# Second attention's rotary partners by DMA, first attention's reciprocals, slab quarters and parts in other places

## The chip, the cores and the metric

The kernel runs on one core of a Trainium2 chip, in one launch. The metric is the time on the device in microseconds (us): the median of three runs was 1079.1 us (1078.55 to 1080.32).

## The reference

Two blocks are computed on 256 tokens of width 1024, in float32. The first has a token mixer (sparse attention with a key selector, 8 heads, beside a short gated convolution), layer norms and a SwiGLU; its shifts, scales and gates come from `c_act @ w_ada`, a vector times a 1024x6144 matrix. The second has two layers: a gated linear attention, then a differential attention, each followed by a SwiGLU and a gated projection. The two places that the change touches:

```python
# first block, attention of the token mixer (8 heads, keys and values shared)
logits = jnp.where(valid, einsum('bqhd,bqkd->bhqk', q_b, kg) * attn_scale, NEG_INF)
p = softmax(logits); out = einsum('bhqk,bqkd->bqhd', p, vg)

# second block, layer 1: differential attention, 8 heads of 2 x 64
q = rms_norm(q.reshape(b, s, nh, 2, dh), g_q)          # k alike
q = rope(q), k = rope(k)                               # x1*cos - x2*sin, x2*cos + x1*sin
s = einsum('bhtqd,bhtkd->bhtqk', q_blk, kt) * dh ** -0.5
pr = softmax(s); a = pr[:, :, 0] - lam * pr[:, :, 1]
o = einsum('bhqk,bhkd->bhqd', a, vt)
```

## The kernel before

Activations lie transposed in SBUF: 128 features on the partitions, 256 tokens along the row, so 1024 features are eight tiles of 128x256. A weight matrix comes in *slabs* of 128x4096 words (2 MB), over two raw buffers. Most projections are made in three products: `split` on ScalarE (line 890) copies a quarter of a slab into the rounded type (`whi`), `low` on VectorE (line 1458) subtracts that from the raw slab (`wlo`), and `three` on TensorE (line 2217) multiplies high by high, high by low and low by high. A slab of four tiles is 96 matmuls.

Each engine has one program, written out by hand in order, and the engines meet at semaphores alone. `me.next(sem)` waits for one more count of a semaphore, `wait_ge` for a count, `banks.claim(bank, sem)` on TensorE waits until the last reader of a PSUM bank is done. There is no planner: what stands behind a waiting instruction on its engine waits too. SyncE's queue loads weights in the order of the phases, with the loads of `behind` (line 672) between them, in order.

**First attention (the head loop at lines 1717 to 1739 on VectorE, 1103 to 1117 on ScalarE, 2517 to 2532 on TensorE).** For head i TensorE makes the scores of head i+1, then one tile of another projection (`in_hc` in heads 0 to 3, `in_gb` in heads 4 to 7), transposes the probabilities of head i (`turned`), multiplies them with the values of head i-1, and sometimes sums columns for the modulation. VectorE does `masked_maxima` (mask, row maxima), ScalarE the exponentials with their sums, VectorE the reciprocals (`invert_sums`), ScalarE the scaling. Between these VectorE has filling work: the convolution of a tile, `low` quarters of the slabs of `out0`, and `modulate_part(n)`, which multiplies a 128x1024 part of `w_ada` (512 KB) into an accumulator. The parts' buffers are reused: in SyncE's order the load of part 20 waits until part 18 is used up (line 638, `part_used` at 19), and behind part 20 stand `load_out(1)`, the second slab of `out0`, and parts 21 to 23. The first quarter of that slab is split by ScalarE in head 5, ahead of its copy of the transposed probabilities.

**Second attention.** `diff_q` and `diff_k` are two slabs each; a slab gives two *pairs* r of tiles (r = 0 to 7; 0 to 3 are q). VectorE takes each tile out of PSUM (line 1997), ScalarE squares a pair (line 1371), TensorE sums the squares over each half of 64 partitions (`block_sums`, line 2767, a 128x512 float32 matmul), ScalarE makes the root (`roots`), VectorE normalizes (line 2122). The rotary partner of a row is 32 partitions away: `partners` (line 2773) multiplies the pair with a signed permutation `rot_d` into PSUM. GpSimd multiplies the pair with the cosines (line 859), and VectorE in `turn(r)` multiplies the partners with the sines and adds (lines 2128, 2132). `partners(r-2)`, `partners(r-1)` and their turns stand one slab later, behind tiles 1 and 3; the last two stand in the middle of the first value tile.

Then a loop over eight heads runs beside the value projection (`value_steps`, three matmuls each, line 2812 to 2862): scores of head i+1, attend(i-2), six value steps, transposes(i-1). VectorE makes maxima, probabilities and `low` quarters, ScalarE exponentials, copies and `split` quarters (`ahead`, line 1429); `ahead(*OUT2, 0)` waits until the second value tile is done.

Of the kernel before, what the change touches and what calls it, by code (L numbers as in the profile page):

```python
# [24 lines left out]
ALU = mybir.AluOpType  # L25
# [39 lines left out]
def column_of(rows):  # L65
    at, n = {}, 0
    for name, k in rows:
# [9 lines left out]
CONSTS = [("ident", P), ("rot_q", P), ("rot_i", P), ("cos_q", T), ("sin_q", T), ("cos_i", T), ("sin_i", T),  # L77
          ("causal", 3 * P), ("blk", P), ("rot_d", P), ("cos_d", T), ("sin_d", T), ("gla_mask", 2 * P)]
COL_C, NC = column_of(CONSTS)
# [3 lines left out]
def shape_constants():  # L83

    out = np.zeros((P, NC), np.float32)

    def put(name, a):
        out[:, COL_C[name]:COL_C[name] + a.shape[1]] = a

    p = np.arange(P)  # L90
    put("ident", np.eye(P))
    put("blk", (p[:, None] // HD == p[None, :] // HD) * 1.0)
    pos = np.arange(T, dtype=np.float32)
    for tag, width, half, theta in (("q", HD, 8, 500000.0), ("i", ID, 8, 500000.0), ("d", HD, 32, 10000.0)):
# [9 lines left out]
        put("rot_" + tag, rot)  # L104
# [168 lines left out]
def build(nc, a, out):  # L273

    ctx = ExitStack()
    with ctx:
# [110 lines left out]
        d_sq, d_rs = sb("d_sq", 1024, at=U + 8192), sb("d_rs", 1024, at=U + 9216)  # L387
        d_t1, d_t2 = sb("d_t1", 512, at=U + 10240), sb("d_t2", 512, at=U + 10752)
        d_nsq = sb("d_nsq", 2048, at=U)
# [6 lines left out]
        def sem(name):  # L396
# [56 lines left out]

        qk_src, qk_sq, qk_stat, qk_sd, qk_normed, qk_cos, qk_rot, qk_rot_read, qk_ready = (
            sem("qk_src"), sem("qk_sq"), sem("qk_stat"), sem("qk_sd"), sem("qk_normed"), sem("qk_cos"),
            sem("qk_rot"), sem("qk_rot_read"), sem("qk_ready"))
        out_done, out_read, last_read, stored = sem("out_done"), sem("out_read"), sem("last_read"), sem("stored")
# [411 lines left out]
        def _(act):  # L869
# [491 lines left out]
            root(X[0], T + 2, 1.0 / D, 1, rstd[:, :])  # L1361
            take_projection(3)
            for base, name in ((0, "diff_q"), (4, "diff_k")):
                def after(at, t, base=base):
                    buf = d_q if base == 0 else d_k
                    if t % 2 == 1:
                        r = base + 2 * at.i + t // 2
# [21 lines left out]
            for q in range(4):  # L1389
                ahead(*VALUES, q)  # L1390
            take_values(0)

# [8 lines left out]
            for i in range(NH + 1):  # L1401
# [24 lines left out]
                if i in (2, 5, 7):  # L1426
                    take_values({2: 1, 5: 2, 7: 3}[i])
                if 1 <= i <= 4:
                    ahead(*OUT2, i - 1)
            wait(act, tile_done, PH["diff_v"].tile0 + 4)  # L1430
# [24 lines left out]
        def _(dve):  # L1455
# [259 lines left out]

            PARTS_OF_HEAD = ((11, 12), (13, 14), (15, 16), (17, 18), (19, 20), (21,), (22,), (23,))
            me.again()
            masked_maxima(0)
            for q in range(2):
                low(PH["out0"], At(0), q)  # L1720
            modulate_part(10)
            for i in range(NH):
                invert_sums(i)
                if i + 1 < NH:
# [3 lines left out]
                if i == 7:  # L1728
                    mix_low(0, 1)
                if i in (1, 2):  # L1730
                    low(PH["out0"], At(0), i + 1)
                if i < 4:
                    short_conv(i)
                else:
                    gated_conv(i - 4)
                    if i in (5, 6):
                        low(PH["out0"], At(1), i - 5)
                for n in PARTS_OF_HEAD[i]:
# [386 lines left out]
            def turn(r):  # L2125
                me.next(qk_rot)
                me.again(qk_ready)
                me.did(dve.tensor_tensor(v3(d_t2[:, :], 2), v3(X[2 + r % 2][:, :], 2), bc(C("sin_d", T), 2), ALU.mult),
                       qk_rot_read)
                me.next(qk_cos)  # L2130
                me.again(qk_rot_read)
                me.did(dve.tensor_tensor(pair(r), d_t1[:, :], d_t2[:, :], ALU.add), qk_ready)

# [12 lines left out]
            low(*VALUES, 0)  # L2146
            low(*VALUES, 1)
            turn(6)
            turn(7)
            make_tile = group_make(d_o, d_nsq, lambda t: lam[:, 5:6])  # L2150
# [10 lines left out]
            for i in range(NH + 3):  # L2161
                if i < NH:
                    me.next(score_done)
                    s = 4 * (i % 2)
                    for c in range(2):
                        me.did(dve.tensor_reduce(neg_max[:, s + 2 * c:s + 2 * c + 2],
                                                 v3(G[2 * (i % 2) + c][:, :], 2), AX, ALU.max, negate=True))
                    me.again()
                    me.did(dve.tensor_scalar(neg_max[:, s:s + 4], neg_max[:, s:s + 4], HD ** -0.5, None, ALU.mult),
                           max_ready)  # L2170
                if i >= 3:
# [22 lines left out]
                if i in (0, 1):  # L2194
                    low(*VALUES, 2 + i)
                if 2 <= i <= 5:
                    low(*OUT2, i - 2)
            for g in range(1, 4):
# [14 lines left out]
        def _(pe):  # L2213
# [554 lines left out]

            def partners(r):
                banks.claim(X[2 + r % 2], qk_rot_read)  # L2770
                pe.wait_ge(qk_normed, r + 1)
                src = tl(d_q, 2 * r, 2) if r < 4 else tl(d_k, 2 * r - 8, 2)
                pe.matmul(X[2 + r % 2][:, :], C("rot_d"), src, start=True, stop=True).then_inc(qk_rot, 1)  # L2773

            start = next_operand()
            for base, name in ((0, "diff_q"), (4, "diff_k")):
                def after(at, t, base=base):
                    r = base + 2 * at.i
                    if r == 0 and t == 1:
                        stats(tok=True)  # L2780
                    if t == 1 and r:
                        partners(r - 2)
                    if t == 3:
                        if r:
                            partners(r - 1)
                        block_sums(r)
# [19 lines left out]

            value_steps(0, 8)
            partners(6)
            partners(7)
            value_steps(8, 16)  # L2810

# [88 lines left out]
```

## Time and profile before

| | |
|---|---|
| median of 3 runs | 1079.1 us (1078.55 to 1080.32) |
| profiled execution, its own time | 1077.96 us |
| its span | 1076.2 us |
| TensorE (PE) busy | 1042.4 us, 97% |
| VectorE (DVE) busy | 731.7 us, 68% |
| ScalarE (ACT) busy | 552.9 us, 51% |
| GpSimd (POOL) busy | 202.2 us, 19% |
| mean granted TensorE clock | 0.995 |

The span is the time from the first to the last instruction of that execution. Rows of a timeline give an instruction's start and its length in us, its engine, line and operands, how many like it are merged, and in brackets how long the engine sat idle before and what ended that. PEld is the weight load of TensorE; SPq and ACTq are DMAs issued by SyncE and ScalarE. Each float32 matmul stands as two records.

### The profile page before, as it was taken

How to read it: one execution, taken by the hardware profiler on the slowest of the kernel's cores; microseconds unless marked ns; L12 is line 12 of the kernel's file. 1: busy time of each engine (PE TensorE's matmuls, PEld its weight loads, DVE VectorE, ACT ScalarE, POOL GpSimd, SP SyncE). 2: the span in 40 equal slices, each digit the busy share in tenths (PEclk: the TensorE clock that was granted, in tenths of full speed). 3: DMA queues.
4: the chain of work that ended last, by engine and by line, in shares of the span. 5: the costliest groups of instructions: out<-in, count | busy, mean ns of one | idle time of the engine just before them, and what ended most of it. 6: DMA issues, size and time to landing. Idle time of an engine off the chain costs nothing.

```text
span 1076.2 us, 20430 instructions
## 1 busy us (share of the span) xinstructions
PE 1042.4 (97%) x7993; PEld 981.9 (91%) x7993; DVE 731.7 (68%) x1155; ACT 552.9 (51%) x946; POOL 202.2 (19%) x223
## 2 busy tenths in 40 slices
PE   5999999999999999999999999999989999999998
PEld 5577788999999998989999999998877999999998
DVE  5798777767654788868556555686787765564565
ACT  2223457545363585527454444566467764544453
POOL 0000012233311001022333321021210223322010
PEclk9999999999999999999999999999999999999999
DMA  9993453577556454504564546654322265644661
GB/s 350 399 389 121 169 184 98 195 254 262 174 168 190 137 192 173 183 2 153 186 209 156 174 131 203 247 185 157 131 105 79 93 222 178 212 132 140 185 208 40
DMA packets 183587, 192.78 MB, mean 179 GB/s; under 512 B 5913, under 2 KB 143426, under 8 KB 183522
## 3 DMA queue, kind: packets, MB, share of 16 engines
q1 hardware_dynamic: 182512, 191.15, 52.5%
q8 instruction: 43, 0.70, 0.3%
q0 software_dynamic: 144, 0.52, 0.2%
q10 hardware_dynamic: 866, 0.21, 0.1%
q14 instruction: 22, 0.18, 0.0%
HBM read 190.83 MB, written 1.05 MB: 178 GB/s over the span
## 4 chain that ended last, share of the span: by engine, by line
PE 56%; DVE 5%; ACT 3%; issue 1%; POOL 0%; DVEq 0%; POOLq 0%; ACTq 0%
PE gemm L2219 17%; PE gemm L2221 17%; PE gemm L2220 16%; DVE wlo L1464 1%; PE aux L2717 1%; PE aux L2835 1%; PE aux L2767 1%; ACT whi L899 1%; DVE prod L1943 1%; PE gemm L2820 1%; PE aux L2773 0%; PE aux L2219 0%; DVE state L2075 0%; PE aux L2221 0%; PE aux L2220 0%
## 5 line engine op out<-in xcount | busy, mean ns | idle before, releaser
L2219 PE MATMUL gemm<-ohi,whi 128*128 128x256 f32 x1376 | 389.5, 283 | 3.8 <-issue 1.1
L1464 DVE TENSOR_TENSOR wlo<-raw,whi 128x1024 fp32r<-128x1024 f32 (+1 forms) x308 | 352.2, 1187 | 58.8 <-ACT whi L899 58.1
L2220 PE MATMUL gemm<-olo,whi 128*128 128x256 f32 x1376 | 385.8, 280 | 0.0
L2221 PE MATMUL gemm<-ohi,wlo 128*128 128x256 f32 x1376 | 383.6, 279 | 0.0
L899 ACT ACTIVATE whi<-raw 128x1024 fp32r<-128x1024 f32 (+1 forms) x308 | 276.4, 963 | 60.4 <-PE gemm L2221 44.2
L2219 PEld LDWEIGHTS gemm<-ohi,whi 128*128 128x128 f32 x1376 | 259.1, 188 | 6.7 <-DVE wlo L1464 2.8
L2220 PEld LDWEIGHTS gemm<-olo,whi 128*128 128x128 f32 x1376 | 259.5, 189 | 0.6 <-issue 0.5
L2221 PEld LDWEIGHTS gemm<-ohi,wlo 128*128 128x128 f32 x1376 | 259.4, 189 | 0.0
L2221 PE MATMUL gemm<-acthi,wlo 128*128 128x256 f32 x528 | 147.8, 280 | 0.0
L2219 PE MATMUL gemm<-acthi,whi 128*128 128x256 f32 x528 | 147.5, 279 | 0.0
L2220 PE MATMUL gemm<-actlo,whi 128*128 128x256 f32 x528 | 147.3, 279 | 0.0
L755 POOL TENSOR_TENSOR prod<-sg,ut 128x256 f32<-128x256 f32 x66 | 51.2, 777 | 265.1 <-DVE ut L1888 161.0
L2220 PEld LDWEIGHTS gemm<-actlo,whi 128*128 128x128 f32 x528 | 99.3, 188 | 0.0
L2221 PEld LDWEIGHTS gemm<-acthi,wlo 128*128 128x128 f32 x528 | 99.1, 188 | 0.0
L2219 PEld LDWEIGHTS gemm<-acthi,whi 128*128 128x128 f32 x528 | 98.8, 187 | 0.0
L1194 ACT ACTIVATE sg<-gt 128x256 f32<-128x256 f32 x66 | 27.6, 419 | 132.9 <-DVE gt L1888 91.4
L759 POOL TENSOR_TENSOR actlo<-prod,acthi 128x256 f32 (+1 forms) x63 | 70.3, 1116 | 0.0
L2220 PE MATMUL gemm<-xlo,whi 128*128 128x256 f32 x224 | 62.6, 279 | 0.0
L1888 DVE TENSOR_TENSOR ut<-gemm,rstd 128x256 f32<-128x256 f32 x44 | 18.4, 418 | 52.1 <-PE gemm L2221 52.1
L782 POOL TENSOR_TENSOR sq_sum<-sq_sum,dsq 128x256 f32<-128x256 f32 x28 | 24.0, 856 | 111.3 <-ACT dsq L924 99.2
L2220 PEld LDWEIGHTS gemm<-xlo,whi 128*128 128x128 f32 x224 | 42.2, 188 | 1.9 <-issue 1.9
L2448 PE MATMUL gemm<-om,raw 128*128 128x256 f32 x192 | 43.6, 383 | 0.0
(383 smaller groups left out, 1549.0 us busy)
## 6 DMA issues: line engine op xcount, KB each, us to landing
raw<-in_ffn_w_in SPq DMA_DIRECT2D x44, 1024.0 KB, 6.2
raw<-in_ffn_w_out SPq DMA_DIRECT2D x32, 704.0 KB, 5.2
part<-in_w_ada SPq DMA_DIRECT2D x32, 512.0 KB, 10.7
raw<-in_gla_w_in SPq DMA_DIRECT2D x6, 2048.0 KB, 7.8
raw<-in_diff_w_in SPq DMA_DIRECT2D x6, 2048.0 KB, 7.9
raw<-in_w_gate SPq DMA_DIRECT2D x11, 1024.0 KB, 6.3
raw<-in_w_up SPq DMA_DIRECT2D x11, 1024.0 KB, 8.5
raw<-in_w_down SPq DMA_DIRECT2D x16, 704.0 KB, 5.2
```

The costliest lines, as they stand in the source:

```text
L755: pool.tensor_tensor(tl(prod, j), tl(sg, j), tl(ut, j), ALU.mult).then_inc(prod_done, 1)
L759: pool.tensor_tensor(tl(actlo, t - 1), tl(prod, 1 - j), tl(acthi, t - 1).bitcast(F32), ALU.subtract).then_inc(actlo_ready, 1)
L782: pool.tensor_tensor(sq_sum[:, :], sq_sum[:, :], src, ALU.add).then_inc(squares_summed if last else sq_added, 1)
L899: act.activation(whi[hslot][:, q * w:(q + 1) * w], src[:, q * w:(q + 1) * w], ACT.Copy).then_inc(hi_ready, 1)
L1194: act.activation(tl(sg, j), tl(gt, j), ACT.Silu).then_inc(silu_done, 1)
L1464: dve.tensor_tensor(wlo[hslot][:, q * w:(q + 1) * w], src[:, q * w:(q + 1) * w], whi[hslot][:, q * w:(q + 1) * w].bitcast(F32), ALU.subtra ...
L1888: ins = dve.tensor_tensor(dst, bank[:, 0:T], rstd[:, 0:T], ALU.mult)
L1943: me.link(dve.tensor_tensor(tl(prod, t % 2), tl(sg, t % 2), pp(k, t), ALU.mult))
L2219: pe.matmul(dst, st_hi, mv_hi, start=start, stop=False)
L2220: pe.matmul(dst, st_hi, mv_lo, start=False, stop=False)
L2221: return pe.matmul(dst, st_lo, mv_hi, start=False, stop=stop_)
L2448: ins = pe.matmul(G[t][:, 0:T], w[:, k, t * P:(t + 1) * P], tl(om, k), start=k == 0, stop=k == KT - 1)
```

## The change

1. `partners` and the matrix `rot_d` go. For each pair r ScalarE issues four DMAs of 32 partitions x 512 words (64 KB each) that copy the pair from SBUF to SBUF with neighbouring groups of 32 partitions exchanged; the sign moves into the table of sines. Pairs r-2 and r-1 are moved behind the first tile of the next slab, pairs 6 and 7 behind the second quarter of the last value slab's `ahead`. VectorE's `turn` waits for the DMA and multiplies in SBUF.
2. In the second attention the maxima of head 0 stand between `turn(6)` and `turn(7)`; the quarters of the first slab of `out2` are split in heads 2 to 5 (before 1 to 4) and their low parts made in heads 3 to 6 (before 2 to 5).
3. In the first attention `invert_sums(i+1)` stands behind head i's convolution or gate, where `invert_sums(i)` stood at the start of head i; that of head 0 stands between the two quarters before the loop. The third quarter stays out of head 1 and goes to head 2, the fourth from head 2 to head 4. From part 12 on, each part up to 20 is made one place later: heads 0 to 7 make (11), (12, 13), (14, 15), (16, 17), (18, 19), (20, 21), (22), (23), where they made (11, 12), (13, 14), (15, 16), (17, 18), (19, 20), (21), (22), (23).

```diff
+            def move_partners(r):
+                src = tl(d_q, 2 * r, 2) if r < 4 else tl(d_k, 2 * r - 8, 2)
+                act.wait_ge(qk_normed, r + 1)
+                if r >= 2:
+                    act.wait_ge(qk_ready, r - 1)
+                for b in range(4):
+                    act.dma_start(d_rot[r % 2][32 * b:32 * b + 32, :], src[32 * (b ^ 1):32 * (b ^ 1) + 32, :]).then_inc(
+                        qk_moved[r % 2], 16)
...
+                    if t == 0 and base + at.i:
+                        for r in (base + 2 * at.i - 2, base + 2 * at.i - 1):
+                            move_partners(r)
...
             for q in range(4):
                 ahead(*VALUES, q)
+                if q == 1:
+                    move_partners(6)
+                    move_partners(7)
...
-                if 1 <= i <= 4:
-                    ahead(*OUT2, i - 1)
+                if 2 <= i <= 5:
+                    ahead(*OUT2, i - 2)
...
-            PARTS_OF_HEAD = ((11, 12), (13, 14), (15, 16), (17, 18), (19, 20), (21,), (22,), (23,))
+            PARTS_OF_HEAD = ((11,), (12, 13), (14, 15), (16, 17), (18, 19), (20, 21), (22,), (23,))
             me.again()
             masked_maxima(0)
-            for q in range(2):
-                low(PH["out0"], At(0), q)
+            low(PH["out0"], At(0), 0)
+            invert_sums(0)
+            low(PH["out0"], At(0), 1)
             modulate_part(10)
             for i in range(NH):
-                invert_sums(i)
                 if i + 1 < NH:
                     masked_maxima(i + 1)
...
-                if i in (1, 2):
-                    low(PH["out0"], At(0), i + 1)
                 if i < 4:
                     short_conv(i)
                 else:
                     gated_conv(i - 4)
-                    if i in (5, 6):
-                        low(PH["out0"], At(1), i - 5)
+                if i + 1 < NH:
+                    invert_sums(i + 1)
+                if i in (2, 4):
+                    low(PH["out0"], At(0), 1 + i // 2)
+                if i in (5, 6):
+                    low(PH["out0"], At(1), i - 5)
                 for n in PARTS_OF_HEAD[i]:
                     modulate_part(n)
...
             def turn(r):
-                me.next(qk_rot)
-                me.again(qk_ready)
-                me.did(dve.tensor_tensor(v3(d_t2[:, :], 2), v3(X[2 + r % 2][:, :], 2), bc(C("sin_d", T), 2), ALU.mult),
-                       qk_rot_read)
+                rot = d_rot[r % 2]
+                dve.wait_ge(qk_moved[r % 2], 64 * (r // 2 + 1))
+                me.did(dve.tensor_tensor(v3(rot[:, :], 2), v3(rot[:, :], 2), bc(C("sin_d", T), 2), ALU.mult), qk_turned)
...
             turn(6)
+            maxima(0)
             turn(7)
...
-                if 2 <= i <= 5:
-                    low(*OUT2, i - 2)
+                if 3 <= i <= 6:
+                    low(*OUT2, i - 3)
...
-                    if t == 1 and r:
-                        partners(r - 2)
                     if t == 3:
-                        if r:
-                            partners(r - 1)
                         block_sums(r)
                         block_sums(r + 1)
...
-            value_steps(0, 8)
-            partners(6)
-            partners(7)
-            value_steps(8, 16)
+            value_steps(0, 16)
```

## Rows read from the trace of the kernel before

**Rows 1.** The page, busy time of TensorE

```profile
PE 1042.4 (97%) x7993; PEld 981.9 (91%) x7993; DVE 731.7 (68%) x1155; ACT 552.9 (51%) x946; POOL 202.2 (19%) x223
```

**Rows 2.** Windows: us, busy by engine (PE, PEld, DVE, ACT, POOL), clock, DMA share, GB/s

```profile
806.00:808.00 2.00, 2.00 (x7) 1.46 (x5) 1.96 (x5) 2.00 (x8) 0.00 (x0) 0.50 0.03 8
```

**Rows 3.** Timeline of TensorE, one partner matmul in diff_q

```profile
742.11 1.02 PE L2773 MATMUL aux<-d_q,const 128*128 128x512 f32 x2
742.56 0.68 PE L2219 MATMUL gemm<-dhi,whi 128*128 128x256 f32 x1
743.08 0.28 PE L2220 MATMUL gemm<-xlo,whi 128*128 128x256 f32 x1
743.20 0.28 PE L2221 MATMUL gemm<-dhi,wlo 128*128 128x256 f32 x1
```

**Rows 4.** Timeline of all engines, from the first slab's end to the second's

```profile
734.74 0.63 ACT L1371 ACTIVATE d_sq<-d_q 128x512 f32<-128x512 f32 x1 [0.27 <-DVE d_q L1997]
735.48 0.30 PEld L2767 LDWEIGHTS aux<-d_sq,const 128*128 128x128 f32 x2 [0.60 <-issue]
...
738.03 1.42 DVE L2122 SCALAR_TENSOR_TENSOR d_q<-d_q,cols_b,d_rs 128x512 f32<-128x512 f32 x2 [3.33 <-ACT d_rs L963]
...
743.07 2.34 DVE L1464 TENSOR_TENSOR wlo<-raw,whi 128x1024 fp32r<-128x1024 f32 x2
...
748.61 1.02 PE L2773 MATMUL aux<-d_q,const 128*128 128x512 f32 x2
...
749.27 0.63 ACT L1371 ACTIVATE d_sq<-d_q 128x512 f32<-128x512 f32 x1 [2.85 <-DVE d_q L1997]
749.47 1.88 PE L2767 MATMUL aux<-d_sq,const 128*128 128x512 f32 x4
```

**Rows 5.** ScalarE's DMA issues in its timeline, and KB and us to landing of two transfers

```profile
23.62 0.36 ACTq L987 DMA_DIRECT2D lam_in<-in_diff_lam_q  x1
...
25.01 0.58 ACT L983 ACTIVATE om<-res,mod 128x256 f32<-128x256 f32 x1
...
lam_in<-in_diff_lam_k ACTq DMA_DIRECT2D x2, 32.0 KB, 6.6
...
out<-o_tok SPq DMA_DIRECT2D x4, 256.0 KB, 2.6
```

**Rows 6.** Timeline of all engines, first heads of the second attention

```profile
788.28 0.84 ACT L1385 ACTIVATE d_v<-gemm,rstd 128x256 f32<-128x256 f32 x2 [1.75 <-PE gemm L2221]
...
792.00 0.47 ACT L1409 ACTIVATE d_p<-gemm,neg_max 128x256 f32<-128x256 f32 x1 [2.87 <-DVE neg_max L2169]
...
794.07 1.13 PE L2820 MATMUL gemm<-d_k,d_q 64*128 64x256 f32 x8 [1.32 <-ACT d_p L1409]
...
801.54 1.06 ACT L899 ACTIVATE whi<-raw 128x1024 fp32r<-128x1024 f32 x1 [2.95 <-PE aux L2221]
...
804.57 1.78 PE L2820 MATMUL gemm<-d_k,d_q 64*128 64x256 f32 x8 [1.91 <-ACT d_p L1409]
...
806.27 2.07 PE L2835 MATMUL aux<-d_pt,d_v 128*128 128x256 f32 x4
```

**Rows 7.** TensorE's waits in the whole span: us in total, times, longest

```profile
PE aux L2501 <- ACT logit L1075: 2.8, 3, 1.3
```

**Rows 8.** Timeline of the first attention, heads 3 to 6, and out_w's landing

```profile
117.23 0.17 DVE L1714 RECIPROCAL rsum<-sums 128x2 f32<-128x2 f32 x1
...
117.63 0.47 SPq L657 DMA_DIRECT2D out_w<-in_w_out  x1
...
126.70 1.04 ACT L899 ACTIVATE whi<-out_w 128x1024 fp32r<-128x1024 f32 x1
...
130.57 0.56 DVE L1704 SCALAR_TENSOR_TENSOR logit<-aux,allow 128x384 f32<-128x384 f32 x1
...
133.46 1.10 PE L2333 MATMUL gemm<-mix_sq,const 128*128 128x512 f32 x2 [0.32 <-ACT mix_sq L1069]
...
DMA to landing us min/median/max: 8.7/8.8/9.0
```

More of the change, by code:

```diff
@@ L77 @@
 CONSTS = [("ident", P), ("rot_q", P), ("rot_i", P), ("cos_q", T), ("sin_q", T), ("cos_i", T), ("sin_i", T),
-          ("causal", 3 * P), ("blk", P), ("rot_d", P), ("cos_d", T), ("sin_d", T), ("gla_mask", 2 * P)]
+          ("causal", 3 * P), ("blk", P), ("cos_d", T), ("sin_d", T), ("gla_mask", 2 * P)]
 COL_C, NC = column_of(CONSTS)
@@ L103, in shape_constants @@
                 cos[m], sin[m] = np.cos(ang[d % half]), np.sin(ang[d % half])
-        put("rot_" + tag, rot)
+        if tag == "d":
+            sin *= rot.sum(0)[:, None]
+        else:
+            put("rot_" + tag, rot)
         put("cos_" + tag, cos)
@@ L387, in build @@
         d_sq, d_rs = sb("d_sq", 1024, at=U + 8192), sb("d_rs", 1024, at=U + 9216)
-        d_t1, d_t2 = sb("d_t1", 512, at=U + 10240), sb("d_t2", 512, at=U + 10752)
+        d_t1 = sb("d_t1", 512, at=U + 10240)
+        d_rot = [sb(f"d_rot{i}", 512, at=place["ohi"] + 512 * i) for i in range(2)]
         d_nsq = sb("d_nsq", 2048, at=U)
@@ L452, in build @@
             sem("u_read"), sem("go_done"), sem("go_read"), sem("gated"))
-        qk_src, qk_sq, qk_stat, qk_sd, qk_normed, qk_cos, qk_rot, qk_rot_read, qk_ready = (
+        qk_src, qk_sq, qk_stat, qk_sd, qk_normed, qk_cos, qk_turned, qk_ready = (
             sem("qk_src"), sem("qk_sq"), sem("qk_stat"), sem("qk_sd"), sem("qk_normed"), sem("qk_cos"),
-            sem("qk_rot"), sem("qk_rot_read"), sem("qk_ready"))
+            sem("qk_turned"), sem("qk_ready"))
+        qk_moved = [sem("qk_moved0"), sem("qk_moved1")]
         out_done, out_read, last_read, stored = sem("out_done"), sem("out_read"), sem("last_read"), sem("stored")
@@ L2125, in turn @@
             def turn(r):
-                me.next(qk_rot)
-                me.again(qk_ready)
-                me.did(dve.tensor_tensor(v3(d_t2[:, :], 2), v3(X[2 + r % 2][:, :], 2), bc(C("sin_d", T), 2), ALU.mult),
-                       qk_rot_read)
+                rot = d_rot[r % 2]
+                dve.wait_ge(qk_moved[r % 2], 64 * (r // 2 + 1))
+                me.did(dve.tensor_tensor(v3(rot[:, :], 2), v3(rot[:, :], 2), bc(C("sin_d", T), 2), ALU.mult), qk_turned)
                 me.next(qk_cos)
-                me.again(qk_rot_read)
-                me.did(dve.tensor_tensor(pair(r), d_t1[:, :], d_t2[:, :], ALU.add), qk_ready)
+                me.again(qk_turned)
+                me.did(dve.tensor_tensor(pair(r), d_t1[:, :], rot[:, :], ALU.add), qk_ready)
             for base, name in ((0, "diff_q"), (4, "diff_k")):
@@ L2147, in _, with maxima @@
             low(*VALUES, 1)
+            def maxima(i):
+                me.next(score_done)
+                s = 4 * (i % 2)
+                for c in range(2):
+                    me.did(dve.tensor_reduce(neg_max[:, s + 2 * c:s + 2 * c + 2],
+                                             v3(G[2 * (i % 2) + c][:, :], 2), AX, ALU.max, negate=True))
+                me.again()
+                me.did(dve.tensor_scalar(neg_max[:, s:s + 4], neg_max[:, s:s + 4], HD ** -0.5, None, ALU.mult),
+                       max_ready)
             turn(6)
+            maxima(0)
             turn(7)
@@ L2161, in _ @@
             for i in range(NH + 3):
[L2162 to L2170, printed above, removed]
+                if 1 <= i < NH:
+                    maxima(i)
                 if i >= 3:
@@ L2767, in block_sums @@
                 pe.matmul(X[r % 2][:, :], C("blk"), tl(d_sq, r % 2, w=512), start=True, stop=True).then_inc(qk_stat, 1)
[L2769 to L2773, printed above, removed]
             start = next_operand()
```

## Prediction, made before the change was run

> **What bounds the kernel now.** I read the page first, for the share of each engine: TensorE is busy for 97% of the span [rows 1], so work taken off TensorE counts in full unless something else becomes late, and anything put between its instructions costs in full. Second, TensorE's waits: where it stands still, there is something to win or to lose. Third, the timelines of the three stretches that the change touches: the first attention (85 to 140 us), the projections of q and k (734 to 780 us) and the heads of the second attention (788 to 834 us). Last the windows, for the granted clock. The reader is to see four things.
>
> A partner product costs TensorE 0.86 us. It starts at 742.11 and the second product behind it at 743.08 [rows 3]. Products follow each other at 0.12 us (743.08 to 743.20), so without it the second would start at 742.23: a difference of 0.85.
>
> The second attention has two stalls on TensorE, 1.32 and 1.91 us, both for ScalarE's exponentials [rows 6]. Behind the longer one the clock is at 0.50, 1.2 instead of 2.4 GHz [rows 2], and the scores take 1.78 us where they took 1.13, the product with the values 2.07 us [rows 6].
>
> The first attention has three stalls, 2.8 us together, in which TensorE waits for scaled probabilities [rows 7].
>
> And in the first attention there is a chain that costs nothing today only because it just arrives: part 18 is used up at 117.23, the second slab of `out0` is issued behind part 20's load at 117.63, lands 8.7 to 9.0 us later, at 126.3 to 126.6, and ScalarE splits it at 126.70 [rows 8].
>
> **Partners by DMA.** Eight products go: 8 x 0.855 = 6.8 us. Not all of it is kept. At the end of a slab the second `block_sums` needs the squares of the pair that ended last. In the first slab it starts 0.11 us behind the end of the squares (734.74 + 0.63 = 735.37, then 735.48) [rows 4]. In later slabs the partner product covers this: tile 3 ends at 748.61, the squares at 749.27 + 0.63 = 749.90, and the sums run from 749.47 on without a wait [rows 4]. Without the cover the first sum takes 748.61 to 749.47 and the second waits until 750.01, 0.54 us. That happens in three slabs, 1.6 us. Left: 6.8 - 1.6 = 5.2 us.
>
> What the DMAs add. ScalarE issues 32 of them at about 0.36 us each [rows 5]; eight in a slab are 2.9 us. The instruction before an issue may still be running: a DMA that stands behind four activations is issued at 23.62, while the last of them runs at 25.01 [rows 5]. So the issues begin when VectorE has normalized the first of the two pairs (738.03 + 0.71, 4.6 us after the slab's end at 734.1 [rows 4]), beside the first two split quarters of 1.0 us each, and end at about 7.6 us; there the third quarter starts. VectorE takes that quarter at 743.07 [rows 4], 9.0 us after the slab's end, so nothing is late. This cover is 0.4 us; if the issues take longer or begin only when the quarters are done, the third starts at 9.2 us, VectorE is up to 1.2 us late, and in three slabs 3.6 us are lost. VectorE turns a pair behind the fourth quarter, at 743.07 + 2.34 [rows 4], 11.3 us after the slab's end. No copy from SBUF to SBUF is in the trace. Nearest from below is the store of 256 KB with 2.6 us, from above the 32 KB with 6.6 us in the saturated start [rows 5]. I take 2.6 us, from the row with idle engines; in the slabs 11.3 us are enough for 6.0 + 2.6 as they are, and for the first pair nearly with 6.6 too. Behind the last slab it matters: pair 6 is issued 4.6 to 6 us after the slab's end and its turn can come at 8.7, behind two quarters; with 2.6 us it lands in time, with 6.6 us everything up to the first exponentials is about 4 us later, and some 2 to 4 of these reach TensorE.
>
> The Trainium skill, "DMA: Bandwidth & Descriptors", section "Issuing engines are not separate DMA queues", says that DMAs issued by ScalarE and SyncE run on the same 16 engines and interleave. By that rule the last two moves share with the 2 MB that SyncE issues about 5 us earlier; its effect lies inside the bounds above.
>
> **Quarters and maxima of the second attention.** `ahead(*OUT2, 0)` waits for the second value tile, until 801.54, and holds back the exponentials of head 2, for which TensorE stands 1.91 us [rows 6]. Moved behind these, it holds back nothing: the exponentials of head 2 can run when their maxima are there. The stall goes, and with it the slow clock: 1.78 - 1.13 and 2.07 - 1.13, 1.6 us; I take 1.5. What is late next: with the partner products gone TensorE reaches the scores at 782.8 (5.35 us earlier), the scores of head 1 need the bank of the first value tile, and ScalarE's copy of it (788.28 [rows 6]) now stands behind eight issues and two splits and ends at 785.4. TensorE waits some 1.6 us there, in place of the 1.32 us at 794.07. The exponentials of head 0 start at about 786.4 instead of 792.00, since the maxima no longer wait for `turn(7)`. From head 3 on TensorE is 8.0 to 8.4 us earlier than before; VectorE, with 4.9 us per head against TensorE's 4.7, keeps up, since it has lost its wait for the split. The low quarters one head later delay the second slab of `out2` by nothing (that load waits for the value slab) and the next feed-forward load not beyond its old time. Sum of the second attention: 5.2 + 1.9 + 1.5, less 0.3 for the changed first stall and 0.3 for waits of ScalarE and VectorE = **-8.0 us**. From below -9.5 (no new stalls), from above -4 (slow copies or 2.9 us of issues uncovered).
>
> **Reciprocals, quarters and parts of the first attention.** TensorE no longer waits in heads 0 to 3: the reciprocal stands a whole head ahead. By head 5 that brings it 3.5 us forward (2.8 us of waits and about 0.2 us around each). But part 18, on which the second slab of `out0` depends, moves from the second place of head 3 to the first of head 4. Ahead of it stand now, besides what stood there, the maxima of head 5 (1.1 us), the gate (0.35), the wait for the exponentials of head 5, since the reciprocal follows a short gate (0.7), two more reciprocals (0.2) and 0.7 us of VectorE's waits for a TensorE that is no longer late: 117.2 + 3.1 = 120.3. The slab's load is issued at 120.7 and lands at 129.5 with the 8.8 us of [rows 8]. ScalarE comes to the split at 125.4 and stands for 4 us; behind it stand its copy of head 5's probabilities and the scaling of head 6. VectorE stands at the low quarter of the same slab and has behind it two parts instead of one. Split until 130.6 (1.04 us [rows 8]), low until 131.9 (1.17 us [rows 4]), parts 20 and 21 until 134.8, then the maxima of head 7, which began at 130.57 [rows 8]. Exponentials, squares of the gated tiles, sums: 137.6 instead of 133.46 [rows 8]. So the first attention ends 4.0 us later, with the 3.5 us gained in it already spent. TensorE stands from 128.3 to 132.0 and from 133.3 to 137.6; a wait of 1.9 us was enough for the slow clock, and there it lasted over 3 us, from the scores at 804.57 to 808 [rows 2, 6], which is half as much in lost work: I take 1.7 us more. Nothing later in the kernel gives this back: TensorE is busy without a break from there to the layer norm. Sum: **+5.7 us**; from below -3.5 (the load arrives in time), from above +8.
>
> The smaller table of constants (64 KB less) and VectorE's product, which reads SBUF in place of PSUM, I put at nothing; both are under 0.2 us.
>
> **Sum.** 1077.96 - 8.0 + 5.7 = 1075.7 us for the profiled execution. The median of the runs is 1.1 us above that execution, so 1076.8 us for the median. A measurement of this kernel can tell about 0.2%, 2.2 us, from no change; the forecast is 2.3 us faster and lies at that bound.
>
> **The rivals.**
>
> *The late slab does not hold anything up (1068 us).* Then the first attention gives its 3.5 us: -8.0 - 3.5 = -11.5, so 1067.6. For it: the three waits [rows 7] really go. Against it: the load is bound to part 18 by SyncE's order, and today it has under half a microsecond to spare [rows 8].
>
> *The moves are late or the issues hold ScalarE up (1080.8 us).* From the point at which a copy takes over 4 us, pair 6 is late for `turn(6)`, all maxima and exponentials of the heads shift, and where the issues lie in front of the third quarter uncovered, 3.6 us go in the slabs. Either takes 4 of the 8 us, and with +5.7 the kernel is slower: 1079.1 - 4 + 5.7 = 1080.8. For it: 6.6 us for 32 KB [rows 5]. Against it: that row is from a time with saturated DMA engines.
>
> *The clock falls again, in the second attention or for longer in the first (1079 us).* TensorE stands 1.6 us behind the first scores, between 1.32 us that cost no clock and 1.91 us that did [rows 6]; price 1.5 us, and a longer slow stretch in the first attention another 1 us: 1076.8 + 2.5 = 1079.3.
>
> *The change does not do what it says*, in that the moved partners or the wait at head 2 stay on the path: the trace would show products of line 2773 or the 1.91 us wait; the code leaves no room for either.
>
> **How the numbers follow.** The forecast has 0.45; with its own range of 1074 to 1079 it is faster by over 0.2% in 0.25, the same in 0.17, slower in 0.03. The first rival has 0.22, faster. The late moves have 0.17: slower in 0.13, same in 0.04. The clock has 0.16: same in 0.07, slower in 0.09. Faster 0.47, same 0.28, slower 0.25. The range from 1067.5 to 1082 holds all cases but the ends of the first and third.
>
> **What would show it.** Right: no products of the rotation; `block_sums` with a wait of about 0.5 us for the squares in three slabs; the 1.91 us wait and the clock of 0.50 at 806 us gone; a wait of ScalarE for `out_w` of about 4 us in head 5, a wait of TensorE for it behind, and a clock of 0.50 around 138 us. Wrong: `out_w` issued at about 117 us or landing before ScalarE comes to it; a `turn` that waits for its DMA; the first attention ending earlier than before.

## The result and the profile after

The changed kernel takes 1086.4 us (median of 4 runs, 1085.35 to 1087.87), the kernel before 1078.8 us beside it. The ratio is 1.0071, 95% interval 1.0058 to 1.0084: 0.7% slower. The forecast was 1076.8 with a range up to 1082, so both the sign and the range were wrong. One run of a later kernel (e10 below) took 5175.8 us; it is left out of that kernel's ratio.

The page of the changed kernel, its busy times and the chain that ended last:

```profile
PE 1039.1 (96%) x7977; PEld 980.2 (90%) x7977; DVE 733.8 (68%) x1155; ACT 552.5 (51%) x946; POOL 202.1 (19%) x223
...
PE 53%; DVE 6%; ACT 4%; ACTq 2%; issue 1%; DVEq 0%
```

The waits of TensorE in the two edited stretches (us in total, times, longest; the first two rows from the heads of the first attention, the others from the second attention):

```profile
PE gemm L2362 <- ACT mix_sq L1074: 4.4, 1, 4.4
PE aux L2530 <- ACT logit L1080: 3.4, 1, 3.4
...
PE aux L2796 <- ACT d_sq L1390: 5.0, 6, 1.2
PE gemm L2836 <- ACT d_v L1404: 4.3, 1, 4.3
```

TensorE has less work than before [rows 1] (7977 records against 7993: the eight partner products, of two records each, are gone) and the kernel is longer: new waits have replaced it. The three waits of [rows 7] are gone, and so is the 1.91 us of [rows 6]. What is new on the chain is ACTq, ScalarE's own issues of DMAs, with 2% of the span, some 20 us of chain (0% on the page of the kernel before).

To see where the 7.4 us of span (1076.2 to 1083.6) arise I followed the lag at fixed places of the program. The weight load that SyncE issues at 83.89 us before goes out at 85.51 after: 1.6 us, ahead of any edited instruction. The last transposes of the first attention lag 6.8 us; the first tile of `diff_q` 5.6 (1.2 us were given back on the way, in small steps between 185 and 300 us, in code that the change does not touch; the trace of e3 below, whose first attention is the same, gives nothing back there); the last product with the values 7.6, the end 7.4. So: 1.6 early, 5.2 in the first attention, 1.2 back, and 2.0 in the second attention, which was to give 8.0.

The timeline of the changed kernel in the first attention (start, length, engine, line, operands, count, idle time before and its cause):

```profile
122.30 0.47 SPq L662 DMA_DIRECT2D out_w<-in_w_out  x1
131.03 1.06 ACT L904 ACTIVATE whi<-out_w 128x1024 fp32r<-128x1024 f32 x1 [4.11 <-DMA out_w<-in_w_out]
132.12 1.22 DVE L1486 TENSOR_TENSOR wlo<-out_w,whi 128x1024 fp32r<-128x1024 f32 x1 [6.23 <-ACT whi L904]
133.30 0.52 PE L2530 MATMUL aux<-const,logit 128*128 128x128 f32 x3 [3.36 <-ACT logit L1080]
136.14 0.56 DVE L1726 SCALAR_TENSOR_TENSOR logit<-aux,allow 128x384 f32<-128x384 f32 x1
139.03 2.05 PE L2362 MATMUL gemm<-mix_sq,const 128*128 128x512 f32 x2 [4.42 <-ACT mix_sq L1074]
```

Against [rows 8] the slab of `out0` is issued 4.7 us later (1.6 of them were there at 85 us already); ScalarE stands 4.1 us for it, VectorE behind it, and TensorE twice. The sums took 1.10 us and take 2.05: the slow clock.

The same view for one slab of the second attention, from the first slab's sums to the second's:

```profile
740.22 1.99 PE L2796 MATMUL aux<-d_sq,const 128*128 128x512 f32 x4 [0.38 <-ACT d_sq L1390]
744.42 0.61 ACTq L1376 DMA_DIRECT2D d_rot<-d_q  x1
744.98 1.04 ACT L904 ACTIVATE whi<-raw 128x1024 fp32r<-128x1024 f32 x1
748.26 1.76 ACTq L1376 DMA_DIRECT2D d_rot<-d_q  x2
750.07 2.01 ACT L904 ACTIVATE whi<-raw 128x1024 fp32r<-128x1024 f32 x2 [4.05 <-issue]
751.16 2.36 DVE L1486 TENSOR_TENSOR wlo<-raw,whi 128x1024 fp32r<-128x1024 f32 x2 [2.41 <-ACT whi L904]
754.66 1.10 PE L2796 MATMUL aux<-d_sq,const 128*128 128x512 f32 x2 [1.16 <-ACT d_sq L1390]
756.72 2.05 PE L2796 MATMUL aux<-d_sq,const 128*128 128x512 f32 x2 [0.96 <-ACT d_sq L1390]
```

The eight issues run from 744.42 to 750.02, 5.6 us, partly beside the first two splits, and the third quarter waits 4.05 us for them ("issue": it waited for no other engine). VectorE then has both last quarters, the third tile and the turn in one heap, the squares are late and TensorE waits twice. The sums start 14.4, 16.0 and 15.0 us apart in the three slabs; before it was 14.9, 14.7 and 14.7 with the partner products between them.

All issues of the moves, as a group (ns min/median/max), and their landing:

```profile
L1376 ACTq DMA_DIRECT2D d_rot<-d_q x16: 515/612/1117, 744.4 to 765.4; - x16
L1376 ACTq DMA_DIRECT2D d_rot<-d_k x16: 514/612/1520, 776.0 to 796.3; - x16
DMA to landing us min/median/max: 2.0/2.1/3.0
```

An issue takes 0.61 us in the median, not the 0.36 of [rows 5]; the copy is on time but for one turn, for which VectorE waits 0.8 us. At the end of the last slab the same happens ahead of the values (ScalarE, then TensorE):

```profile
796.96 2.00 ACT L904 ACTIVATE whi<-raw 128x1024 fp32r<-128x1024 f32 x2 [4.36 <-issue]
798.87 0.82 ACT L1404 ACTIVATE d_v<-gemm,rstd 128x256 f32<-128x256 f32 x2
799.84 2.08 PE L2836 MATMUL gemm<-d_k,d_q 64*128 64x256 f32 x8 [4.33 <-ACT d_v L1404]
```

The granted clock in windows of the changed kernel (columns as in [rows 2]) is 0.50 from 798 to 804 us, TensorE having stood still from 795.5:

```profile
798.00:800.00 2.00, 0.16 (x2) 0.20 (x3) 1.86 (x4) 2.00 (x6) 0.72 (x1) 0.50 0.00 0
802.00:804.00 2.00, 2.00 (x10) 2.00 (x11) 1.93 (x7) 0.52 (x3) 0.00 (x0) 0.50 0.00 0
```

### The profile page after: what moved, and what is told of

It reads as the page before. It is cut to its first block, busy times and chain, and to the rows that moved or that the text cites. A ratio compares the mean times of both kernels' runs of the same rounds, so it can differ in the third digit from the quotient of the medians.

```text
span 1083.6 us, 20418 instructions
## 1 busy us (share of the span) xinstructions
PE 1039.1 (96%) x7977; PEld 980.2 (90%) x7977; DVE 733.8 (68%) x1155; ACT 552.5 (51%) x946; POOL 202.1 (19%) x223
## 4 chain that ended last, share of the span: by engine, by line
PE 53%; DVE 6%; ACT 4%; ACTq 2%; issue 1%; DVEq 0%
PE gemm L2248 15%; PE gemm L2250 15%; PE gemm L2249 15%; DVE wlo L1486 2%; ACTq L1376 2%; ACT whi L904 1%; PE aux L2746 1%; PE aux L2851 1%; PE gemm L2836 1%; PE aux L2248 1%; PE aux L2796 1%; DVE prod L1967 1%; PE aux L2250 1%; PE aux L2249 1%; DVE state L2099 0%
## 5 line engine op out<-in xcount | busy, mean ns | idle before, releaser
L2477 PEld LDWEIGHTS gemm<-om,raw 128*128 128x128 f32 x192 | 36.5, 193 | 8.5 <-issue 3.8
## 6 DMA issues: line engine op xcount, KB each, us to landing
part<-in_w_ada SPq DMA_DIRECT2D x32, 512.0 KB, 10.4
```

The source lines that it names most:

```text
L2477: ins = pe.matmul(G[t][:, 0:T], w[:, k, t * P:(t + 1) * P], tl(om, k), start=k == 0, stop=k == KT - 1)
```

## Experiments

Every kernel was timed against the kernel before on the same chip; ratios are with their 95% intervals. "Second attention" is the time in its profile from the first tile of `diff_q` to the last product with the values; it repeats within 1.1 us where the code of that stretch is the same.

| kernel | us | ratio to before | second attention |
|---|---|---|---|
| before | 1078.8 | 1 | 103.5 |
| after | 1086.4 | 1.0071 | 105.5 |
| e1 second attention only | 1081.6 | 1.0015 | 105.9 |
| e2 first attention only | 1085.2 | 1.0064 | 103.5 |
| e3 half the issues | 1077.5 | 0.9992 | 96.1 |
| e4 moves by SyncE | 1075.7 | 0.9977 | 95.2 |
| e5 old parts | 1079.7 | 1.0006 | 105.5 |
| e6 late parts on before | 1083.5 | 1.0041 | 103.5 |
| e7 quarters, maxima on before | 1075.3 | 0.9964 | 99.7 |
| e8 e4 and e5 | 1069.2 | 0.9908 | 95.1 |
| e9 e8, norm behind gate | 1069.9 | 0.9917 | 95.1 |
| e10 slab before part 20 | 1083.1 | 1.0034 | 104.9 |
| e11 double issues | 1109.0 | 1.0277 | 128.8 |
| e12 e9, low quarters later | 1067.9 | 0.9896 | 95.1 |

**e1 and e2: the halves of the change.** e1 has the edits of the second attention alone, e2 those of the first.

> The second attention's edits alone (moves by DMA, maxima, quarters of out2); the first attention as in the kernel before. Theory A: the two stretches are independent, and the second attention is a small loss: from the first tile of diff_q to the last head the changed kernel lost 2.0 us more (5.6 us behind at diff_q's first tile, 7.6 behind at the last product with the values), so this kernel is 2 us slower than before, 1080.8 us. If the 1.6 us that the changed kernel was behind already at 85 us come from the smaller table of constants, they show here too: 1082.4. Rival B: the second attention gains its 8 us when it is alone, and the loss came from the two together: 1071.

> The first attention's edits alone (reciprocals, quarters, parts); partners on TensorE, maxima and out2's quarters as before. Theory A: 5.6 us slower at diff_q's first tile less the 1.6 us that were there at 85 us, ahead of any edited instruction: 4.0 us slower, 1082.8; if these 1.6 us come from this part of the change, 5.6 us slower, 1084.4. Rival: the delay is given back later in the kernel, 1079 to 1080.

e1: 1081.6 us, 1.0015 (1.0002 to 1.0027), second attention 105.9. e2: 1085.2, 1.0064 (1.0051 to 1.0078), second attention 103.5. The halves add up (0.15% + 0.64% against 0.71%), rival B falls, and the first attention's delay is still there at the end: e2's span is 5.9 us longer than that of before. The early 1.6 us belong to neither: e6, with the table of constants of before, has them (its load goes out at 85.25), and e3, with the smaller table, has not (83.80). In these kernels they go with the granted clock from 35 to 45 us. Four kernels in that window, in order before, after, e6, e3:

```profile
35.00:45.00 10.00, 8.81 (x30) 5.12 (x31) 6.58 (x13) 4.03 (x6) 0.00 (x0) 0.83 1.05 412
```
```profile
35.00:45.00 10.00, 8.81 (x27) 4.67 (x26) 6.58 (x13) 3.99 (x5) 0.00 (x0) 0.66 1.05 410
```
```profile
35.00:45.00 10.00, 8.81 (x25) 4.67 (x25) 6.67 (x13) 3.99 (x5) 0.00 (x0) 0.66 1.05 411
```
```profile
35.00:45.00 10.00, 8.81 (x30) 5.03 (x30) 6.67 (x13) 4.11 (x6) 0.00 (x0) 0.83 1.05 411
```

In e5, e8, e10 and e11 the load is late too (84.87 to 85.46) with 0.83 to 1.00 in that window. There a group of 32 products that starts at 24.2 to 24.4 us takes 10.1 to 11.4 us in place of 8.43, while the clock column shows 1.00; why, the traces do not show. So this time comes and goes in code that is the same, and it needs no edit. Whether the change makes it more frequent is open: one of the four profiled executions with the old table has it, and eight of the ten with the smaller one.

**e3: half the issues, the same bytes.**

```diff
-                src = tl(d_q, 2 * r, 2) if r < 4 else tl(d_k, 2 * r - 8, 2)
+                src = tl(d_q, 2 * r, 4) if r < 4 else tl(d_k, 2 * r - 8, 4)
...
-                    act.dma_start(d_rot[r % 2][32 * b:32 * b + 32, :], src[32 * (b ^ 1):32 * (b ^ 1) + 32, :]).then_inc(
-                        qk_moved[r % 2], 16)
+                    act.dma_start(d_rot_both[32 * b:32 * b + 32, :], src[32 * (b ^ 1):32 * (b ^ 1) + 32, :]).then_inc(
+                        qk_moved[0], 16)
...
-                        for r in (base + 2 * at.i - 2, base + 2 * at.i - 1):
-                            move_partners(r)
+                        move_partners(base + 2 * at.i - 2)
```

> The changed kernel with both pairs of a slab moved by the same four DMAs (32 partitions x 1024 words, 128 KB) in place of eight of 64 KB: half the issues, the same bytes. Theory A: what holds the third quarter of a slab back is ScalarE's time for issues, 0.61 us each and 4.9 us for eight; with four the third quarter starts 2.4 us earlier in each slab, the waits for squares fall from 5.0 us to about 1.6 and the wait of 4.3 us ahead of the scores of head 1 to about 2, with less slow clock: 6 to 8 us faster than the changed kernel, 1079 to 1080. Rival C: an issue takes twice as long for twice the bytes, or the waits come from the partner product's missing cover alone: within 1 us of the changed kernel, 1086.

1077.5 us, 0.9992 (0.9983 to 1.0001): 8.9 us faster than the changed kernel, a little more than expected. Second attention 96.1. An issue of twice the bytes costs the same, and the waits for squares are 1.6 us in four:

```profile
L1377 ACTq DMA_DIRECT2D d_rot<-d_q x8: 515/612/620, 745.6 to 761.2; - x8
```
```profile
PE aux L2795 <- ACT d_sq L1390: 1.6, 4, 0.4
PE gemm L2835 <- ACT d_v L1404: 1.5, 1, 1.5
```

**e11: twice the issues, the same bytes.**

```diff
-                for b in range(4):
-                    act.dma_start(d_rot[r % 2][32 * b:32 * b + 32, :], src[32 * (b ^ 1):32 * (b ^ 1) + 32, :]).then_inc(
+                for b in range(8):
+                    act.dma_start(d_rot[r % 2][16 * b:16 * b + 16, :], src[16 * (b ^ 2):16 * (b ^ 2) + 16, :]).then_inc(
```

> The changed kernel with each move cut into eight DMAs of 16 partitions (32 KB) in place of four of 64 KB: 64 issues, the same bytes. Theory A: ScalarE pays about 0.6 us for each issue, whatever its size (e3: 0.61 for 128 KB); 16 issues between the second and the third quarter are 9.8 us, the third quarter starts 4.9 us later in three slabs, and the scores of head 1 wait 4.9 us longer for ScalarE's copy: 20 us slower than the changed kernel, 1104 to 1110. Rival C: the time goes with the bytes: 1086 to 1088.

1109.0 us, 1.0277 (1.0263 to 1.0291), second attention 128.8: 22.6 us slower than the changed kernel, as expected. ScalarE's third quarter in the first slab:

```profile
758.01 2.00 ACT L904 ACTIVATE whi<-raw 128x1024 fp32r<-128x1024 f32 x2 [9.75 <-issue]
```

With 0, 16, 32 and 64 issues on ScalarE (e4, e3, after, e11) the second attention takes 95.2, 96.1, 105.5 and 128.8 us: the first 16 are nearly free, the next cost 0.6 us each and more, since the cover is used up. One detail was not as expected: the wait ahead of the scores (8.0 us) was for the turned pair, not for ScalarE's copy.

**e4: the same moves issued by SyncE.**

```diff
+                      ("diff_k", 0): moves(0, 1), ("diff_k", 1): moves(2, 3),
+                      ("diff_v", 0): moves(4, 5), ("diff_v", 1): moves(6, 7),
```

> The changed kernel with the same 32 DMAs issued by SyncE, each group of eight behind the weight load that is issued at the same slab's end. Theory A: ScalarE's queue is free again, so the third quarter starts as before; the second attention gives the forecast's 8 us in place of a loss of 2: 10 us faster than the changed kernel, 1076 to 1078. Rival C: the moves' landing or the missing cover is the cause, and it stays at 1084 to 1086. Rival D: SyncE comes late to the next weight load behind its eight issues: a new wait of ScalarE for a slab, 1080 to 1086.

1075.7 us, 0.9977 (0.9968 to 0.9986): 10.7 us faster than the changed kernel. Second attention 95.2, that is 8.3 us less than before; the forecast was 8.0. SyncE's issues take as long (0.59 us), but nothing urgent stands behind them. One slab of e4:

```profile
743.62 2.94 ACT L916 ACTIVATE whi<-raw 128x1024 fp32r<-128x1024 f32 x3
745.92 3.96 SPq L683 DMA_DIRECT2D d_rot<-d_q  x5
748.27 2.34 DVE L1482 TENSOR_TENSOR wlo<-raw,whi 128x1024 fp32r<-128x1024 f32 x2
752.95 1.02 PE L2792 MATMUL aux<-d_sq,const 128*128 128x512 f32 x2
754.38 1.10 PE L2792 MATMUL aux<-d_sq,const 128*128 128x512 f32 x2 [0.41 <-ACT d_sq L1389]
```

The splits run through, the low quarters start at 748.27 instead of 751.16 though the slab began only 0.4 us earlier, and of the waits for squares the 0.41 us remain that the missing partner product uncovers (0.54 were forecast). Rival D does not decide: ScalarE waits 1.8 us for slabs in two places, and TensorE for none of it. The Trainium skill, "DMA: Bandwidth & Descriptors", section "Issuing engines are not separate DMA queues", says that issuing from several engines saves only the time to initiate a DMA, "which is usually small relative to the DMA itself". The trace agrees that the issuing time is what is saved, but here it is not small: the eight issues of a slab took 5.6 us beside a landing of 2.1, and the choice of the issuing engine alone is worth 10.7 us.

**e7: maxima and `out2`'s quarters alone.**

```diff
-                if 1 <= i <= 4:
-                    ahead(*OUT2, i - 1)
+                if 2 <= i <= 5:
+                    ahead(*OUT2, i - 2)
...
             turn(6)
+            maxima(0)
             turn(7)
```

> The kernel before with only the maxima of head 0 ahead of turn(7) and out2's quarters one head later; partners on TensorE. Theory A: the 1.91 us stall and its slow clock go, 3.4 us, less 0.3: 1075.7. Rival F: another wait takes the stall's place (low quarters against the maxima on VectorE): 1078 to 1079.

1075.3 us, 0.9964 (0.9951 to 0.9976): as expected. Second attention 99.7, 3.8 us less than before. The rest of e4's 8.3 us, 4.5, is what the partner products gave (5.2 forecast). Its profiled execution met a slow clock in code of the first attention that it shares with the kernel before, which cost it some 3 us there:

```profile
115.00:125.00 10.00, 10.00 (x34) 7.34 (x35) 6.04 (x12) 3.12 (x9) 0.00 (x0) 0.66 0.59 202
```

**e5, e6, e10: why the first attention is later.** e5 is the changed kernel with the parts in their old heads, e6 the kernel before with the new ones, and e10 the changed kernel with one change in SyncE's order:

```diff
-                      ("in_gb", 0): [*parts(18, 19, 20), lambda: load_out(1), *parts(21, 22, 23)],
+                      ("in_gb", 0): [*parts(18, 19), lambda: load_out(1), *parts(20, 21, 22, 23)],
```

> The changed kernel with the parts in the heads in which they were before (part 18 in head 3 again); reciprocals and quarters stay in their new places. Theory A: the first attention's loss comes only from part 18 used up late (121.9 us), since the second slab of out0 is issued behind it; with part 18 back the slab is issued at about 117 us, the 4 us wait of ScalarE for it and TensorE's waits of 3.4 and 4.4 us go, and the 3.5 us of the earlier reciprocals are kept: 7 to 8.5 us faster than the changed kernel, 1078 to 1079. Rival E: VectorE has too much ahead of the maxima in heads 3 and 4 whatever part is there, and half of the loss stays: 1082.

> The kernel before with the parts of the changed kernel only: each part one place later, reciprocals and quarters as before. Theory A: the load of the second slab of out0 goes late by one part and what stands ahead of it, 3 us or more, and the row of the kernel before has 0.4 us to spare: 4 to 7 us slower than before, 1083 to 1086 (more than with the early reciprocals, whose 3.5 us are missing here). Rival E: late only together with the early reciprocals: 1079 to 1080.

> The changed kernel with one change in SyncE's order: the load of the second slab of out0 stands ahead of the load of part 20, not behind it, so it no longer waits until part 18 is used up, only until part 17 is. The parts stay in their new heads, VectorE's and ScalarE's programs are untouched. Theory A: the loss in the first attention is the order of the loads: the slab is issued at 116.9 us instead of 122.3, ScalarE's 4.1 us wait for it goes, and the time is that of the old parts, 1079 to 1081. Rival E: VectorE's work moved to later heads is what makes the maxima late, and the load only seemed to: 1084 to 1086.

e5: 1079.7 us, 1.0006 (0.9997 to 1.0015), 6.7 us less than the changed kernel: a little short of theory A (7 to 8.5). e6: 1083.5, 1.0041 (1.0025 to 1.0057), slower by 4.2 without any early reciprocal; its profiled execution has the slow clock between 115 and 125 us that e7's has, and behind it ScalarE's wait for the slab (3.3 us) and one of 4.3 us on TensorE for the scaled probabilities. Its runs lie between 1080.4 and 1087.1 us, half of them under 1082, and the trace is one of the longer ones: how much of the 4.2 us is that slow clock is open. e10: 1083.1, 1.0034 (1.0022 to 1.0046), between the theories: 3.3 us less than the changed kernel, 3.4 more than e5. So the loss has two halves, about equal within the intervals. One is the load behind part 18, as forecast. The other comes with the new places of the parts; the trace puts it down mostly to VectorE's second part in head 5, which stands ahead of the maxima of head 7 when the slab is on time too: behind the same low quarter the parts take from 130.10 to 132.95 us in e10 and from 129.08 to 130.61 in e5. TensorE's wait in e10 and in e5:

```profile
PE gemm L2362 <- ACT mix_sq L1074: 3.8, 1, 3.8
```
```profile
PE gemm L2362 <- ACT mix_sq L1074: 2.6, 1, 2.6
```

And in e5, where the slab is on time and the parts are as before, 2.6 us remain (0.3 before). In its trace, counted from 85 us, the last transposes of the first attention come 0.4 us later than before: all of the 3.5 us that the reciprocals bring is taken back by then. By the medians (0.5 us slower, with 2.0 lost in the second attention) some 1.5 us are kept. What takes the rest back is the wait for the squares, behind VectorE's maxima of head 7, and the slow clock after it.

**e8, e9, e12: the mends together.** e8 is e4 with the old parts. e9 puts `mix_norm(0, 1)` behind the gate and the reciprocal of head 6. e12 has e9's order and

```diff
-                if i in (5, 6):
-                    low(PH["out0"], At(1), i - 5)
+                if i in (6, 7):
+                    low(PH["out0"], At(1), i - 6)
```

> The changed kernel with both mends: moves issued by SyncE and part 18 back in head 3. Theory A: 8 us less in the second attention and 3.5 us less in the first than before: 1066 to 1069. If the mends don't add up, because the time won in the first attention is lost to the loads in between: 1070 to 1072.

> The kernel of e8 with VectorE's mix_norm(0, 1) (two instructions, 1.7 us) behind the gate and the reciprocal of head 6 instead of ahead of them. In e5 and e8 TensorE still stood 2.6 and 2.8 us for the squares of the gated tiles, which VectorE delivers behind the maxima of head 7 and mix_norm. Theory A: this is what of the earlier reciprocals' 3.5 us was not kept; with mix_norm behind, the squares come 1.7 us earlier, the wait is 0.9 to 1.1 us and the slow clock behind it goes: 2 to 3.5 us less than e8, 1065.5 to 1067. Rival: mix_norm's own reader (the high parts on ScalarE) comes late in its turn and holds the transposes: no gain, 1069.

> The kernel of e9 with VectorE's first two low quarters of the second slab of out0 one head later (heads 6 and 7 in place of 5 and 6). In e9 the wait of 2.6 us stayed, since ScalarE's squares stand behind the exponentials of head 7 (130.96 to 131.85) and these wait for maxima that begin at 129.72, behind the wait for the split (2.0 us), the low quarter (1.2) and part 21 (1.5). Theory A: with the low quarter out of head 5, part 21 is the only thing ahead of the maxima; it lands 5.4 us after its issue at 121.26, so the maxima begin at about 128.3, 1.4 us earlier, the wait falls to about 1.2 us and the slow clock behind it (1.7 us in e9) goes: 3 us less than e9, 1066 to 1067. Rival: the low quarters are late in heads 6 and 7 in their turn, or the clock stays low: 1069 to 1070, no gain.

e8: 1069.2 us, 0.9908 (0.9894 to 0.9922), where the upper end of theory A was 1069; second attention 95.1. e9: 1069.9, 0.9917 (0.9903 to 0.9931), no gain. The reason was not its rival's but that the squares stand behind the exponentials of head 7, and these behind late maxima. e12: 1067.9, 0.9896 (0.9878 to 0.9915): 2 us less than e9 by the medians (the intervals overlap), with the mechanism in the trace. e9 first, then e12:

```profile
129.72 0.56 DVE L1722 SCALAR_TENSOR_TENSOR logit<-aux,allow 128x384 f32<-128x384 f32 x1
132.61 1.78 PE L2358 MATMUL gemm<-mix_sq,const 128*128 128x512 f32 x2 [2.61 <-ACT mix_sq L1086]
```
```profile
129.70 0.56 DVE L1722 SCALAR_TENSOR_TENSOR logit<-aux,allow 128x384 f32<-128x384 f32 x1
132.59 1.10 PE L2358 MATMUL gemm<-mix_sq,const 128*128 128x512 f32 x2 [1.11 <-ACT mix_sq L1086]
```

The clock times are alike because e12's execution was 1.5 us behind e9's at 85 us; against its own TensorE the maxima come 1.5 us earlier, the wait falls to 1.1 us, and the sums run at the full clock. e12 is the fastest kernel of the study: 1.0% under the kernel before, 1.7% under the changed one.

## Why the prediction was wrong

**The term of the second attention failed, at one step: the duration of ScalarE's issues and their cover.** I took 0.36 us from [rows 5], for a transfer of another kind (a small load at the start of the kernel). It is the shortest of the four issues that stand together in the trace of the kernel before; two of the others:

```profile
24.02 0.49 ACTq L987 DMA_DIRECT2D lam_in<-in_diff_lam_k  x1
24.53 0.45 ACTq L987 DMA_DIRECT2D lam_in<-in_diff_lam_q  x1
```

Eight at 0.36 were to end 7.6 us after the slab's end, with the words "This cover is 0.4 us"; at 0.49 they would have used it up already. They take 0.61 us in the median, eight take 5.6, and the third quarter starts 10.4 us after the slab's end (739.7 to 750.07), 2.8 later than forecast. The working did name the case, "if the issues take longer or begin only when the quarters are done, the third starts at 9.2 us", and priced it at 3.6 us in three slabs; for the heads it priced only a late landing. Measured it is more: e4 against after is 10.4 us in the second attention (10.7 in the medians). Of these 3.4 are waits for squares (5.0 in six places against 1.6 in four) and 3.3 the wait ahead of the scores (4.3, against one of 1.0 for the exponentials in e4). The other 3.7 no view puts down to a wait; slow clock behind the waits fits them, since it is granted at 0.76 from 756 to 763 us and at 0.55 from 798 to 805, where e4 has 1.00. I bounded the landing of a move from both sides, by rows; the issue I did not, and it was the one that decided. In all, 32 issues by 0.61 are 19.6 us of an engine whose splits TensorE needs.

**The other steps of it were right, or nearly.** With the issues out of the way the forecast -8.0 is measured as -8.3 (e4), and the whole kernel takes 1075.7 us where 1076.8 was forecast for the changed one. Some of that closeness is luck: the partner products gave 0.7 less than forecast and the quarters and maxima 0.7 more. Landing 2.1 us (2.6 taken). The wait for squares in three slabs 0.41 (0.54). The quarters and maxima -3.8 (forecast -3.4, less 0.3 for the first stall, so -3.1).

**The first attention was right in size and in its chain.** +5.7 forecast, 5.2 in the two traces and 6.4 in e2 by medians. "Nothing later in the kernel gives this back" failed in the trace of the changed kernel, by the 1.2 us. Issue of the slab 122.3 in a trace that is 1.6 us behind from the start, so 120.7, as forecast; ScalarE's wait 4.11 (4); split, low quarter and sums at 129.4, 130.5 and 137.4 in the same count, against 129.5, 130.7 and 137.6; slow clock behind, as forecast. What I had not separated is that the new places of the parts cost about as much as the load (e10).

**The rivals.** "The late slab does not hold anything up" falls: ScalarE stands 4.11 us. It would not have paid its 3.5 us in full either: e5 has the slab on time and TensorE still waits 2.6 us for the next thing that is late. "The moves are late or the issues hold ScalarE up", with 0.17, is what happened, in its second half; its price of 4 us was too small by 6. "The clock falls again" happened as a consequence, inside it.

**The sum by the measured terms:** 1077.96 + 2.0 + 5.2 - 1.2 (given back) + 1.6 (the early time) = 1085.6, against 1085.43 for the profiled execution of the changed kernel.

## What to carry to other kernels

A DMA costs the engine that issues it time, here 0.6 us for 32, 64 and 128 KB alike, and that time stands in the queue of that engine: count issues, not bytes, ask what is next on the issuing engine, and issue from the one on which nothing urgent waits, or fewer and larger. Where a term has an "if it takes longer" in its working, bound that duration from both sides like any other, from all rows of its kind and not from the first, and carry it into the chances. And when work is moved off a late engine by bringing one thing forward, look for the next thing that the same engine delivers late before counting the whole wait as won.

## What the hardware showed that was not expected

An issue of an SBUF-to-SBUF copy takes 0.61 us on ScalarE for 32, 64 and 128 KB alike (0.59 on SyncE), where the small loads beside that of [rows 5] took 0.36 to 0.49 and the 2 MB slab at 122.30 us, by SyncE, 0.47: here the time does not go with the bytes. Single issues took up to 1.5 us after and 1.7 in e11. The copy itself lands in 2.1 us for 64 KB and 2.4 us for 128 KB. And the granted clock can fall in one execution and not in another of the same code: 0.66 (after) or 0.83 (before) between 35 and 45 us (1.6 us), and 0.66 (e7) or 1.00 (before) between 115 and 125 us (3 us), which is as large as the effects that one profile is read for. Medians over several runs and lags against a fixed place of the same trace kept these apart as far as they could; in e6 they did not.
